# Gate blocks of a two-layer hybrid attention encoder: one run of blocks per attention job, or per pair of heads, in place of two

## The chip, the cores and the metric

One core of a Trainium2 chip runs the whole program. The metric is the device time of one execution in microseconds (us), given as the median of several runs. All times below are from the kernel before the change.

## The reference

Two layers (DEPTH = 2) over 640 tokens (512 of a prompt, 8 x 16 of samples with caches), D_MODEL = 1024. Cut to what matters here:

```python
h = rmsnorm(x, g_mix[l])
qa, ka, va, cq, ckv, kpe, ga, gb = jnp.split(h @ w_in[l], SPLIT_IDX, axis=-1)
oa = swa_sink_attention(...)          # branch A, window of 128, 8 heads
ob = mla_attention(...)               # branch B, latent attention, 8 heads
mixed = jax.nn.sigmoid(ga) * (oa @ w_oa[l]) + jax.nn.sigmoid(gb) * (ob @ w_ob[l])
x = x + mixed @ w_out[l]
x = x + (silu(h2 @ w_gate[l]) * (h2 @ w_up[l])) @ w_down[l]    # h2 = rmsnorm(x, g_ffn[l])
```

The columns `ga` and `gb` of the input projection, 2048 in all, are the gates. They depend on `h` alone, so their products can be computed at any time before the merge.

## The kernel before

Everything is float32. A large product is made of three fp32r products of a high and a low part (high x high, high x low, low x high). Tokens are the columns; 640 are taken as two halves of 320. A weight unit (128 output columns, 8 blocks of 128 rows) is loaded by SP into `w_raw`, rounded by ACT into `w_hi` (`high`, line 749), and the rest is left by POOL in `w_lo` (line 701); there are two slots of each. `high` of the next unit waits for `w_started`, which TensorE raises with the first matmul of the unit now in use (line 1347).

A gate group is one weight unit: 8 blocks (k = 0 to 7), each of 6 matmuls of 320 columns (lines 1336 to 1350), accumulated in `acc[:, 0]`. When all 8 blocks are done, `gate_full` lets DVE move the sum out (`gate_out`, line 1932), ACT takes the tanh (line 1009) and SP stores it. TensorE has 16 gate groups per layer. Most of them are cut up by hand and put between the steps of attention jobs, so that TensorE has work while the softmax of a job runs on DVE and ACT. `gate_part(j)` (line 119) says which blocks belong to job j:

- Window jobs (j = 0 to 15, branch A): 8 for the prompt with 4 blocks each, 8 for the samples with 2 blocks each.
- Head jobs (branch B on the prompt, 32 jobs, here numbered 0 to 31 from J_B = 16; job n is head n % 8 of the query tile t = n // 8, with (t + 1) x 128 keys): 2 blocks each in jobs 0 to 15, 1 block each in jobs 16 to 23, none in jobs 24 to 31. A gate group begins at jobs 0, 4, 8, 12 and 16 and ends at jobs 3, 7, 11, 15 and 23. Another whole group stands ahead of job 0.
- Sample jobs of branch B (8 jobs): 1 block each.

A job has four steps on TensorE: `score` (queries by keys, plain float32), `turn` (transposes the probabilities into the one buffer `psT`), the product with the values (`pv`, written in two halves of 64 output columns), and its gate blocks. Between them stand the other engines' steps:

- DVE: maximum of the scores (line 1913), then, when ACT has taken the exponential, the scaling of `probs` (line 1917). Its order is fixed: step n + 1's maximum with step n's scaling, and after the step of job n a `gate_out`, if a gate group ended in job n - 1.
- ACT, in this order for job n: exponential of job n + 1 (line 944), copy of `psT` to `pT` (line 954), copy of a finished output tile (line 959), tanh of an ended gate (line 1009), `high` of the next weight unit if a gate group begins in job n (line 758).

`turn` of job n waits for `probs` of job n and for the `pT` copy of job n - 1 (there is one `psT`). `pv` waits for the `pT` copy. The head jobs go in pairs: `pv_heads` does both jobs of a pair.

For window jobs, `jobs` (line 1352) puts half of a job's blocks ahead of its `pv` and half behind; where a gate group begins in the job, all stand behind `pv`. The sample jobs of branch B use the same function with 1 block: half rounded up is 1, so the block stands ahead of `pv`, or behind it in the first job. For head jobs, `head_jobs` (line 1376) runs, for the pair j and j + 1:

```python
score(j+4); gates(j); turn(j+1); score(j+5); gates(j+1); pv(j, j+1); turn(j+2)
```

Of the kernel before, what the change touches and what calls it, by code (L numbers as in the profile page):

```python
# [118 lines left out]
def gate_part(j):  # L119

    if j < J_SA:
        return 1 + j // 2, 4 * (j % 2), 4
    if j < J_B:
        return 1 + N_CHUNK // 2 + (j - J_SA) // 4, 2 * ((j - J_SA) % 4), 2
    if j < J_B + 2 * H_B:
        return GATE_B + 1 + (j - J_B) // 4, 2 * ((j - J_B) % 4), 2
    if j < J_B + 3 * H_B:
        return GATE_B + 5, j - J_B - 2 * H_B, 1
    if j >= J_SB:
        return GATES - 2, j - J_SB, 1  # L130
    return None
# [14 lines left out]
def gate_unit(g, block=0):  # L146


    if g < GATES_A:
        return N_IN + g  # L150
    return UNIT_GB + g - GATES_A + (g > GATE_SB or (g == GATE_SB and block >= KD // 2))


def gate_acc(g):

    return 1 if g in (GATES_A - 1, GATES - 1) else 0
# [117 lines left out]
def build(nc, io):  # L274
    with ExitStack() as ctx:
# [910 lines left out]
        def _(pe):  # L1186
            def unit_ready(n):
                pe.wait_ge(s_w_lo, n + 1)
# [76 lines left out]
            def score_b(l, j):  # L1265
                if j == J_B + 2:

                    pe.wait_ge(s_evac, l * TILES + (CREDIT + TILE_MERGE))
                if j - 4 >= (J_SB if j >= J_SB else J_B):

                    pe.wait_ge(s_exped, l * JOBS + (j - 3))
                if j < J_SB:
                    t, h = divmod(j - J_B, H_B)
                    last = pe.matmul(score_bank(j)[:, 0:(t + 1) * P], qB[0:QK_B, h, t * P:(t + 1) * P], kB[:, h, 0:(t + 1) * P],  # L1274
                                     start=True, stop=True, skip_group_check=True)
                else:
                    b = j - J_SB
                    cs = b % 4
                    pe.wait_ge(bcache_loaded[cs], l * (32 * DEC_BATCH // 4) + 32 * (b // 4 + 1))
                    pe.wait_ge(s_newcols, l * DEC_BATCH + (b + 1))  # L1280
                    out = score_bank(j)[:, 0:KEYS_B]
                    for a in range(KC):
                        pe.matmul(out, q_lat[:, a, b, :, :], cb_t[:, cs, a, :], start=a == 0, stop=False,
                                  skip_group_check=True)
                    last = pe.matmul(out, q_pe[:, b, :, :], cb_p[:, cs, :], start=False, stop=True, skip_group_check=True)
                last.then_inc(s_scored, 1)

            def turn_b(l, j):
                pe.wait_ge(s_probs, l * JOBS + (j + 1))
                if j >= 1:  # L1290
                    pe.wait_ge(s_pT, l * JOBS + j)
                s = j % 2
                n = (j - J_B) // H_B + 1 if j < J_SB else KC
                for i in range(n):
                    last = pe.transpose(psT[:, i * P:(i + 1) * P], probs[:, s, i * P:(i + 1) * P], ident[:, :])  # L1295
                if j >= J_SB:
                    last = pe.transpose(psT[0:DEC_SEQ, PAST:PAST + P], probs[:, s, PAST:KEYS_B], ident[:, :])
                last.then_inc(s_turned, 1)

            def pv_heads(l, j):  # L1300

                t, h = divmod(j - J_B, H_B)
                pe.wait_ge(s_pT, l * JOBS + (j + 2))
                if h == 0:
                    pe.wait_ge(s_o, l * O_GROUPS + (O_B + t))
                for i in range(t + 1):
                    for s in range(2):
                        r = slice(s * V_B, (s + 1) * V_B)
                        last = pe.matmul(psO[r, (h // 2) * P:(h // 2 + 1) * P], vB[:, i, (h + s) * V_B:(h + s + 1) * V_B],  # L1309
                                         pT[:, s, i * P:(i + 1) * P], start=i == 0, stop=i == t, skip_group_check=True)  # L1310
                        if i == t:
                            last.then_inc(s_pv, 1)
# [17 lines left out]
            def gate_blocks(l, g, blocks):  # L1330

                if blocks[0] == 0:

                    if g > 0:
                        pe.wait_ge(s_gate_evac, l * GATES + (g if gate_acc(g) == gate_acc(g - 1) else g - 1))
                for k in blocks:
                    slot = gate_unit(g, k) % 2
                    new = k == 0 or gate_unit(g, k) != gate_unit(g, k - 1)
                    if new:
                        unit_ready(l * UNITS + gate_unit(g, k))  # L1340
                    whi, wlo = w_hi[:, slot, k * P:(k + 1) * P], w_lo[:, slot, k * P:(k + 1) * P]
                    for w, x, s0, s1 in ((whi, h_hi, k == 0, False), (whi, h_lo, False, False), (wlo, h_hi, False, k == KD - 1)):
                        for half in range(2):
                            last = pe.matmul(acc[:, gate_acc(g), half, 0:HALF], w, x[:, k, half * HALF:(half + 1) * HALF],  # L1344
                                             start=s0, stop=s1)
                            if new:
                                last.then_inc(w_started, 1)
                                new = False
                if blocks[-1] == KD - 1:
                    last.then_inc(gate_full, 1)  # L1350

            def jobs(l, first, last, score, turn, pv, ahead, lead, blocks):
                for j in range(first, first + ahead):
                    score(l, j)

                gate_blocks(l, lead, blocks)
                if first == J_SB:
                    pe.wait_ge(s_sprep_c, l * 8 + 8)
                turn(l, first)
                for j in range(first, last):  # L1360
                    if j + ahead < last:
                        score(l, j + ahead)

                    g, k, n = gate_part(j) or (0, 0, 0)
                    before = (n + 1) // 2 if k else 0
                    if before:
                        gate_blocks(l, g, range(k, k + before))
                    pv(l, j)  # L1370
                    if n > before:
                        gate_blocks(l, g, range(k + before, k + n))
                    if j + 1 < last:
                        turn(l, j + 1)

            def head_jobs(l):

                for j in range(J_B, J_B + 4):
                    score_b(l, j)
                gate_blocks(l, GATE_B, range(KD))  # L1380
                turn_b(l, J_B)
                for j in range(J_B, J_SB, 2):
                    for e in (j, j + 1):
                        if j + 4 < J_SB:
                            score_b(l, e + 4)
                        g, k, n = gate_part(e) or (0, 0, 0)
                        if n:
                            gate_blocks(l, g, range(k, k + n))
                        if e == j:
                            turn_b(l, j + 1)  # L1390
                    pv_heads(l, j)
                    if j + 2 < J_SB:
                        turn_b(l, j + 2)
# [181 lines left out]
            for l in range(DEPTH):  # L1575
# [29 lines left out]
                pe.wait_ge(s_vprep_c, l * 4 + 4)  # L1605
                pe.wait_ge(acache_loaded, l * 32 + 32)
                jobs(l, J_A, J_B, score_a, turn_a, pv_a, 2, 0, range(3, KD))

                pe.wait_ge(s_cq, l * KQ + KQ)
# [47 lines left out]
                pe.wait_ge(s_spread, l * 16 + 16)  # L1657
                pe.wait_ge(s_kcopy, l * (H_B // 2) + H_B // 2)
                head_jobs(l)
                gate_blocks(l, GATE_SB, range(4))  # L1660

# [20 lines left out]

                pe.wait_ge(s_sprep_c, l * 8 + 6)
                jobs(l, J_SB, JOBS, score_b, turn_b, pv_b, 3, GATE_SB, range(6, KD))

                pe.wait_ge(uv_loaded, l * 16 + 16)
# [815 lines left out]
```

## Time and profile before

| | us |
|---|---|
| median of 3 runs | 1847.4 |
| runs | 1844.79 to 1848.89 |
| the profiled execution | 1847.09 |
| its span | 1845.3 |
| TensorE busy in the span | 1773.0 (96%) |
| window jobs with their gates, layer 0 | about 113.8 to 190 |
| head jobs with their gates, layer 0 | about 227 to 308 |
| head jobs, layer 1 | about 1131 to 1212 |

The span runs from the first to the last instruction of the profiled execution. The granted TensorE clock is full in the stretches looked at. Times in the rows are from the start of the span. "x2" after a matmul means two records; a plain float32 matmul leaves two, a transpose and an fp32r matmul one. The rows of 320-column matmuls come in twos, one row for the two halves; the start of a row minus the start of the row before is what the two took. A row's own length is longer than that, because matmuls overlap and their ends are modelled.

### The profile page before, as it was taken

The page shows a single profiled execution, that of the slowest core. Times are in us where ns is not written, and L with a number is a line of the kernel's source. Part 1 is how long each engine was busy: PE and PEld are TensorE (multiplying, and loading weights), DVE is VectorE, ACT ScalarE, POOL GpSimd, SP SyncE. Part 2 cuts the span into 40 slices and gives each one's busy share as a digit, 9 for nine tenths or more (in the row PEclk, how much of TensorE's full clock was granted, in tenths as well). Part 3 has the DMA queues.
Part 4 walks back from the last instruction along what each step waited for, and adds up shares of the span by engine and source line. Part 5 has one row for each costly group of instructions (what it writes and reads, how often), then busy time and mean ns, then how long its engine had stood idle before and what let it go on. Part 6 is the DMA issues. An engine that isn't in the chain of part 4 may idle for free.

```text
span 1845.3 us, 31477 instructions
## 1 busy us (share of the span) xinstructions
PE 1773.0 (96%) x12122; PEld 1695.9 (92%) x12122; DVE 1033.8 (56%) x1590; ACT 705.3 (38%) x1401; POOL 616.5 (33%) x345
## 2 busy tenths in 40 slices
PE   6899998999999999999999999999999999999998
PEld 6898886999989999999999888779999999999997
DVE  4464455475673746547537544545748545647464
ACT  4245345413442424334431643543134323334243
POOL 1322321133243443435233223112333443534432
PEclk9999999999999999999999999999999999999999
DMA  5222522342222121322222235134421231321212
GB/s 183 94 72 106 144 77 90 126 152 88 69 83 89 63 97 58 103 63 89 61 86 73 75 115 136 60 119 143 137 78 60 79 103 54 105 81 64 97 52 86
DMA packets 63786, 171.22 MB, mean 93 GB/s; under 512 B 8120, under 2 KB 13912, under 8 KB 63512
## 3 DMA queue, kind: packets, MB, share of 16 engines
q1 hardware_dynamic: 62808, 167.73, 27.9%
q10 hardware_dynamic: 864, 1.97, 0.3%
q8 instruction: 72, 1.18, 0.3%
q14 instruction: 42, 0.34, 0.1%
HBM read 151.03 MB, written 19.43 MB: 92 GB/s over the span
## 4 chain that ended last, share of the span: by engine, by line
PE 82%; DVE 7%; ACT 4%; issue 3%; POOL 2%; DMA 2%; SPq 1%; POOLq 0%; DVEq 0%; ACTq 0%
PE acc L1499 36%; PE acc L1344 12%; PE acc L1555 11%; PE psU L1555 9%; PE psS L1555 3%; PE psU L1295 1%; PE psU L1309 1%; POOL w_lo L706 1%; PE acc L1274 1%; PE psU L1324 1%; ACT w_hi L758 1%; ACT pT L954 1%; DVE s_lo L1952 1%; POOL w_lo L701 1%; PE acc L1652 1%
## 5 line engine op out<-in xcount | busy, mean ns | idle before, releaser
L701 POOL TENSOR_TENSOR w_lo<-w_raw,w_hi 128x1024 fp32r<-128x1024 f32 x102 | 249.2, 2443 | 696.6 <-ACT w_hi L758 696.6
L758 ACT ACTIVATE w_hi<-w_raw 128x1024 fp32r<-128x1024 f32 (+2 forms) x194 | 174.2, 898 | 449.6 <-PE acc L1499 414.5
L706 POOL TENSOR_TENSOR w_lo<-w_raw,w_hi 128x512 fp32r<-128x512 f32 (+2 forms) x92 | 143.9, 1564 | 340.4 <-ACT w_hi L758 340.4
L2288 DVE TENSOR_TENSOR xT<-acc,xT 128x640 f32<-128x640 f32 x88 | 72.6, 825 | 212.8 <-PE acc L1499 212.7
L1499 PE MATMUL acc<-act_hi,w_hi 128*128 128x320 f32 x694 | 159.4, 311 | 11.6 <-POOL w_lo L706 8.6
L1499 PE MATMUL acc<-act_hi,w_lo 128*128 128x320 f32 x694 | 158.2, 309 | 0.0
L1499 PE MATMUL acc<-act_lo,w_hi 128*128 128x320 f32 x694 | 158.1, 309 | 0.0
L725 POOL TENSOR_TENSOR s_raw<-w_raw 128x512 f32<-128x512 f32 x72 | 105.0, 1458 | 152.6 <-DVE s_lo L1952 110.0
L778 ACT ACTIVATE s_hi<-s_raw 128x512 fp32r<-128x512 f32 x144 | 90.3, 627 | 146.8 <-POOL s_raw L725 53.6
L1952 DVE TENSOR_TENSOR s_lo<-s_raw,s_hi 128x512 fp32r<-128x512 f32 x144 | 112.9, 799 | 48.1 <-ACT s_hi L778 47.7
L1344 PE MATMUL acc<-h_hi,w_hi 128*128 128x320 f32 x512 | 137.2, 349 | 1.2 <-DVE gate L1932 1.2
L1952 DVE TENSOR_TENSOR a_lo<-w_raw,a_hi 128x512 fp32r<-128x512 f32 x108 | 116.9, 1083 | 28.1 <-ACT a_hi L778 27.8
L1499 PE MATMUL acc<-h_hi,w_hi 128*128 128x320 f32 x512 | 120.0, 316 | 11.0 <-POOL w_lo L701 6.7
L1499 PEld LDWEIGHTS acc<-act_hi,w_hi 128*128 128x128 f32 x694 | 115.4, 188 | 14.6 <-POOL w_lo L706 10.7
L1499 PE MATMUL acc<-h_lo,w_hi 128*128 128x320 f32 x512 | 117.2, 310 | 0.0
L1499 PE MATMUL acc<-h_hi,w_lo 128*128 128x320 f32 x512 | 117.2, 310 | 0.0
L1344 PE MATMUL acc<-h_hi,w_lo 128*128 128x320 f32 x512 | 116.5, 309 | 0.0
L1344 PE MATMUL acc<-h_lo,w_hi 128*128 128x320 f32 x512 | 116.4, 308 | 0.0
L1499 PEld LDWEIGHTS acc<-act_hi,w_lo 128*128 128x128 f32 x694 | 115.9, 188 | 0.0
L1499 PEld LDWEIGHTS acc<-act_lo,w_hi 128*128 128x128 f32 x694 | 115.9, 188 | 0.0
L954 ACT ACTIVATE pT<-psU 128x256 f32<-128x256 f32 (+6 forms) x128 | 50.3, 406 | 147.2 <-PE psU L1295 84.8
L1344 PEld LDWEIGHTS acc<-h_hi,w_hi 128*128 128x128 f32 x512 | 84.6, 188 | 21.5 <-issue 10.7
(341 smaller groups left out, 4638.1 us busy)
## 6 DMA issues: line engine op xcount, KB each, us to landing
w_raw<-in_w SPq DMA_DIRECT2D x116, 512.0 KB, 3.5
w_raw<-in_w_pairs SPq DMA_DIRECT2D x72, 512.0 KB, 3.4
w_raw<-in_w SPq DMA_DIRECT2D x48, 256.0 KB, 2.7
gates<-gate SPq DMA_DIRECT2D x32, 320.0 KB, 2.2
tmp<-gates SPq DMA_DIRECT2D x32, 320.0 KB, 3.2
w_raw<-in_w SPq DMA_DIRECT2D x32, 320.0 KB, 2.8
cb_t<-in_cb_t SPq DMA_DIRECT2D x16, 256.0 KB, 3.0
cb_v<-in_cb_v SPq DMA_DIRECT2D x16, 256.0 KB, 2.8
```

Source lines behind the costliest of these rows:

```text
L701: pool.tensor_tensor(w_lo[:, s, :], w_raw[:, s, :], w_hi[:, s, :], ALU.subtract).then_inc(s_w_lo, 1)
L706: pool.tensor_tensor(w_lo[:, n % 2, 0:cols], w_raw[:, n % 2, 0:cols], w_hi[:, n % 2, 0:cols], ALU.subtract).then_inc(s_w_lo, 1)
L725: pool.tensor_tensor(part_raw[o][:, :], x, y, op).then_inc(s_sum, 1)
L758: act.activation(w_hi[:, slot, 0:cols], w_raw[:, slot, 0:cols], ACT.Copy).then_inc(s_w_hi, 1)
L778: act.activation(part_hi[o][:, :], part_source(i, o), ACT.Copy).then_inc(s_part_hi, 1)
L954: last = act.activation(pT[0:rows, j % 2, cols], psT[0:rows, cols], ACT.Copy)
L1274: last = pe.matmul(score_bank(j)[:, 0:(t + 1) * P], qB[0:QK_B, h, t * P:(t + 1) * P], kB[:, h, 0:(t + 1) * P], start=True, stop=True, skip ...
L1344: last = pe.matmul(acc[:, gate_acc(g), half, 0:HALF], w, x[:, k, half * HALF:(half + 1) * HALF], start=s0, stop=s1)
L1499: last = pe.matmul(acc[:, m % 2, half, 0:HALF], w, x[:, half * HALF:(half + 1) * HALF], start=s0, stop=s1)
L1555: last = pe.matmul(out, w, x[:, k, cols], start=fresh and s0, stop=s1, skip_group_check=True)
L1952: dve.tensor_tensor(part_lo[o][:, :], part_source(i, o), part_hi[o][:, :], ALU.subtract).then_inc(s_part_lo, 1)
L2288: then(evac, dve.tensor_tensor(two(xT[:, c, :]), acc2(m), two(xT[:, c, :]), ALU.add), alone=g is None and c == KD - 1)
```

## The change

In window jobs, all blocks of a job stand ahead of its `pv`, except in jobs where a gate group begins, where they stay behind it. In head jobs, both scores of the pair and the turn of the pair's second job come first, and the blocks of both jobs follow as one run ahead of `pv_heads`. The sample jobs of branch B keep their order: with one block, half rounded up is that block.

```diff
@@ jobs @@
                     g, k, n = gate_part(j) or (0, 0, 0)
-                    before = (n + 1) // 2 if k else 0
+                    before = n if k else 0
                     if before:
                         gate_blocks(l, g, range(k, k + before))
                     pv(l, j)
@@ head_jobs @@
                     for e in (j, j + 1):
                         if j + 4 < J_SB:
                             score_b(l, e + 4)
-                        g, k, n = gate_part(e) or (0, 0, 0)
-                        if n:
-                            gate_blocks(l, g, range(k, k + n))
-                        if e == j:
-                            turn_b(l, j + 1)
+                    turn_b(l, j + 1)
+                    parts = [gate_part(e) for e in (j, j + 1) if gate_part(e)]
+                    if parts:
+                        gate_blocks(l, parts[0][0], range(parts[0][1], parts[-1][1] + parts[-1][2]))
                     pv_heads(l, j)
                     if j + 2 < J_SB:
                         turn_b(l, j + 2)
```

A pair of head jobs is then: `score(j+4); score(j+5); turn(j+1); gates(j and j+1); pv(j, j+1); turn(j+2)`. Pairs 24 and 26 have no gates, but their second score now stands ahead of the second turn too.

## Rows read from the trace of the kernel before

**Rows 1.** The page's part 4: the chain that ended last, by engine.

```profile
PE 82%; DVE 7%; ACT 4%; issue 3%; POOL 2%; DMA 2%; SPq 1%; POOLq 0%; DVEq 0%; ACTq 0%
```

**Rows 2.** Timeline, head pair 14, layer 0: start, length, engine, line, operation, tiles.

```profile
267.59 0.45 PE L1344 MATMUL acc<-h_hi,w_lo 128*128 128x320 f32 x2
267.88 0.38 PE L1295 MATMUL psU<-ident,probs 128*128 128x128 f32 x2
268.10 0.81 PE L1274 MATMUL acc<-kB,qB 96*128 96x384 f32 x2
...
269.05 0.45 PE L1344 MATMUL acc<-h_lo,w_hi 128*128 128x320 f32 x2
...
270.21 0.46 PE L1344 MATMUL acc<-h_hi,w_lo 128*128 128x320 f32 x2
270.60 0.66 PE L1309 MATMUL psU<-pT,vB 128*64 128x128 f32 x8
271.19 0.55 PE L1295 MATMUL psU<-ident,probs 128*128 128x128 f32 x3
271.57 0.81 PE L1274 MATMUL psS<-kB,qB 96*128 96x384 f32 x2
```

**Rows 3.** Timeline, window job 1, layer 0: its pv between two runs of gates.

```profile
131.52 0.65 PE L1258 MATMUL psU<-pT,vwin 128*64 128x256 f32 x4
132.10 0.56 PE L1344 MATMUL acc<-h_hi,w_hi 128*128 128x320 f32 x2
132.49 0.45 PE L1344 MATMUL acc<-h_lo,w_hi 128*128 128x320 f32 x2
```

**Rows 4.** Timeline, head pair 0, layer 0, where a gate has just ended.

```profile
228.78 0.28 DVE L1917 TENSOR_SCALAR probs<-probs,rd 128x128 f32<-128x128 f32 x1
...
230.30 2.40 POOL L701 TENSOR_TENSOR w_lo<-w_raw,w_hi 128x1024 fp32r<-128x1024 f32 x1 [5.30 <-ACT w_hi L758]
...
230.72 2.06 DVE L1917 TENSOR_SCALAR probs<-probs,rd 128x128 f32<-128x128 f32 x1
...
232.84 0.33 PE L1295 MATMUL psU<-ident,probs 128*128 128x128 f32 x1
```

**Rows 5.** Timeline, window job 6, layer 0: a unit's first matmul and what follows it.

```profile
159.04 0.56 PE L1344 MATMUL acc<-h_hi,w_hi 128*128 128x320 f32 x2
...
159.55 1.06 ACT L758 ACTIVATE w_hi<-w_raw 128x1024 fp32r<-128x1024 f32 x1 [0.61 <-PE acc L1344]
...
160.69 2.41 POOL L701 TENSOR_TENSOR w_lo<-w_raw,w_hi 128x1024 fp32r<-128x1024 f32 x1 [8.87 <-ACT w_hi L758]
```

**Rows 6.** Timeline, head pairs 4 and 8, layer 0: second job's probs, next turn (its weight load, PEld, in pair 8).

```profile
238.53 0.28 DVE L1917 TENSOR_SCALAR probs<-probs,rd 128x128 f32<-128x128 f32 x1
...
242.79 0.33 PE L1295 MATMUL psU<-ident,probs 128*128 128x128 f32 x1
...
249.05 0.34 DVE L1917 TENSOR_SCALAR probs<-probs,rd 128x256 f32<-128x256 f32 x1
...
253.67 0.20 PEld L1295 LDWEIGHTS psU<-ident,probs 128*128 128x128 f32 x2 [0.35 <-DVE probs L1917]
```

**Rows 7.** Timeline, head pair 16, layer 0: weights, pv, next turn.

```profile
273.27 1.05 ACT L758 ACTIVATE w_hi<-w_raw 128x1024 fp32r<-128x1024 f32 x1
...
275.32 0.88 PE L1309 MATMUL psU<-pT,vB 128*64 128x128 f32 x12 [0.20 <-ACT pT L954]
...
277.19 0.55 PE L1295 MATMUL psU<-ident,probs 128*128 128x128 f32 x3 [1.00 <-DVE probs L1917]
```

**Rows 8.** Timeline, head pair 26, layer 0: no gates.

```profile
297.17 1.02 PE L1274 MATMUL acc<-kB,qB 96*128 96x512 f32 x2
297.37 0.60 ACT L954 ACTIVATE pT<-psU 128x512 f32<-128x512 f32 x1 [0.66 <-PE psU L1295]
...
298.12 0.63 PE L1295 MATMUL psU<-ident,probs 128*128 128x128 f32 x4
...
298.78 0.60 ACT L954 ACTIVATE pT<-psU 128x512 f32<-128x512 f32 x1
...
299.53 1.09 PE L1309 MATMUL psU<-pT,vB 128*64 128x128 f32 x16
```

## The prediction

> **What bounds the kernel now.** I read first the chain that ended last: TensorE holds 82% of it [rows 1], so a microsecond taken from or added to TensorE's own order counts nearly in full, and the other engines matter where TensorE waits for them. Then I read the timeline of the two stages that the change touches, for two questions: what does it cost TensorE to go from one kind of step to another, and what is ready when a step is brought forward?
>
> For the first question take pair 14 [rows 2]. Two matmuls of 320 columns take 0.29. The last two gate matmuls start at 267.59 and the turn at 267.88: leaving the gates for a turn costs nothing. The turn takes 0.22 (two transposes of 0.11). The score starts at 268.10, and the second row of gates at 269.05. Between them lie 0.95: the first two gate matmuls (0.29) and a score of 0.66. At one rate for four passes of 384 columns the score is about 0.64 (that makes 0.11 for 128 columns in a turn's two passes, as seen), so entering the gates from a score costs at most 0.02. Only pv costs: from the last gates (270.21) to pv is 0.39 where 0.29 would do, and from pv to the next turn 0.59 where the products themselves need 0.43. That turn then takes 0.38 to the next score, where three transposes need 0.32.
>
> In the window jobs pv stands between two runs of gates [rows 3]: pv takes 0.58, again 0.15 over its 0.43, and the first two gate matmuls behind it take 0.39, 0.10 too long.
>
> **Count.** A second run of gates disappears in 4 prompt and 6 sample window jobs and in 12 head pairs (0 to 22), 22 per layer, 44 in all. No matmul, transfer or copy is added or removed. SP's loads and stores keep their order and wait for the same signals, later by what is priced below; the next unit is needed about 10 us after its load, which hides that.
>
> **Window jobs: a small gain.** Their turns and scores keep their places; pv moves behind all gates of the job and is followed by a turn instead of gates. Removed: the 0.10 of entering the gates behind pv. Added: about 0.06 of a turn behind pv [rows 2]. The 0.15 behind pv itself stays. That is 0.04 a job; in 9 jobs per layer a turn follows (behind the last job comes another fp32r product, which pays the same entry), so 18 x 0.04 = 0.7 us gained. From below this could be 0; from above, if the whole 0.25 behind pv went, 4.5. I take 0.7, from the rows of the same steps. What covered the softmax is still there: from turn to turn a job has the same work as before, only in another order.
>
> The Trainium skill, page "TensorEngine Tiling (Array Packing)", section "Key Properties", says that a change of tiling mode drains TensorE. By that, pv with its 64-column halves has one change ahead of it and one behind in either order, so the window term would be 0 and the sum 4.6 in place of 3.9. The rows agree that the cost is at pv and not at gates, turns and full-width scores.
>
> **Head jobs: nothing gained, cover lost.** Here the removed boundary was gates to turn, score to gates: 0.02 at most by the rows. What changes is that turn(j+1) loses the 1.76 us (two blocks; 0.88 in jobs 16 to 23) that lay between it and turn(j). It must now wait for the pT copy of job j and for probs of job j+1, with only two scores as cover. Behind the waiting turn queue all gates of the pair and its pv; ACT's next w_hi waits for the first of those gates.
>
> In most pairs the scores suffice. A turn needs about 0.66 to reach the ACT copy at four transposes, the copy is 0.60, and the two scores of 512 columns that stand there take 1.71 [rows 8]; both sides shrink with t. In pair 2, with the shortest scores, up to 0.1 may show; it goes into the range.
>
> Where a gate has just ended, DVE does gate_out ahead of probs(j+1). Pairs 0, 4, 8, 12 and 16 are such.
>
> - Pair 0: probs(1) end at 229.06 [rows 4]. A waiting turn starts 0.06 behind probs (232.78 to 232.84 [rows 4]), so turn(1) starts at 229.12 and the gates at 229.23. Now a second chain: the first matmul of a unit lets ACT make the next w_hi 0.51 later and POOL finish w_lo 4.06 later (159.04 to 163.10 [rows 5]). The scaling of the job after next is held while POOL works: 2.06 instead of 0.28, ending 0.08 behind w_lo [rows 4]. So turn(j+2) comes no earlier than 4.06 + 0.08 + 0.06 = 4.20 behind the first gate: 233.43 instead of 232.84, **0.59** lost.
> - Pair 4: probs(5) end at 238.81 [rows 6], turn(5) 238.87, gates 238.98, turn(6) 243.18 instead of 242.79: **0.39**.
> - Pair 8: probs(9) end at 249.39, turn(9) 249.45, two transposes, gates 249.67. The POOL chain gives 253.87; TensorE's own way, four blocks (3.52), 0.10 to pv and 0.59, gives 253.88, instead of 253.67 [rows 6]: **0.21**. Less than the wait, because turn(10) was waiting 0.35 before.
> - Pair 12: the two scores are 1.28 instead of 0.85, 0.43 more, which covers a wait like pair 8's 0.4: **0**.
> - Pair 16: no wait at the turn: scores from 271.57 [rows 2] take 1.28, turn(17) is at 272.85, the gates begin at 273.18. But w_hi, at 273.27 before [rows 7], now waits until 273.18 + 0.51 = 273.69. Behind it on ACT stand the exponential of job 18 and the pT copy of job 17, so pv(16) and, through w_lo and probs, turn(18) come later by **0.42**. Both already waited [rows 7].
>
> Pair 26 has no gates. Its second score now stands ahead of turn(27): scores from 297.17, each 0.85, end at 298.87, where turn(27) began at 298.12. The copy follows 0.66 behind the turn and takes 0.60 [rows 8], so pT is ready at 300.13, pv starts at about 300.20 instead of 299.53: **0.67**. Jobs 28 to 31 have neither scores nor gates to make it up. In pair 24 ACT reaches the copy late anyway, behind a tanh: 0.
>
> Unknown is a score followed directly by a turn in the other pairs. Nearest is 297.17 to 298.12, 0.95 for 0.85 of work, so 0 to 0.10; but that turn also waited for the copy ending at 297.97. I take 0.
>
> **Sum.** Per layer 0.59 + 0.39 + 0.21 + 0.42 + 0.67 = 2.28, both layers 4.6, less 0.7: +3.9 us. Against the profiled execution's 1847.09 (span 1845.3) this is 1851.0. That execution lies 0.3 below the median of the runs shown, so I put the time at 1851.3. Bounds: the window term at 4.5 leaves +0.1; 0.10 in each of the nine other gated or unpriced pairs (2, 6, 10, 12, 14, 18, 20, 22, 24), both layers, adds 1.8: +5.7.
>
> **Rivals.**
> 1. The lost cover is largely taken up: the w_hi that begins a little later still finds POOL and DVE in time, and only pair 26 counts. 2 x 0.67 - 0.7 = +0.6, 1848.0. For it: turn(10) and turn(18) already waited for probs [rows 6, 7], so part of any delay ahead of them is free. Against: the delay goes into the very chain that they wait for.
> 2. Faster, through one mechanism: each second run of gates costs TensorE a restart like the one behind pv, 0.25, everywhere. 44 x 0.25 = 11.0, less 4.6: 1841.0. It wins from 4.6 / 44 = 0.10 per run. For it: rows 3. Against: in head pairs the rows show 0.02 at most, and 24 of the 44 are there.
> 3. More cover lost: a score directly ahead of a turn costs 0.10 in the nine pairs above: +5.7, 1853.1.
> That the change does nothing is no rival, except in the sample jobs of branch B, where no order changes.
>
> **How the numbers follow.** Forecast 0.62, rival 1 0.16, rival 2 0.08, rival 3 0.14. A measurement can tell about 0.2%, 3.7 us, from no change. The forecast of 3.9 lies on that bound: I count 0.36 of its 0.62 as slower and 0.26 as the same; with rival 3 slower is 0.50, with rival 1 the same is 0.42, faster 0.08. The range, 1846.0 to 1855.0, holds rivals 1 and 3 and the spread of the runs (4 us) at its ends, and leaves out rival 2.
>
> **What would show it.** Right: in pairs 0, 4 and 8 a turn(j+1) waiting 0.3 to 1.3 for probs; w_hi 0.51 behind the first gate in pairs 0 to 16; pv(26) about 0.7 later behind turn(26); window jobs 1, 3, 5 and 7 shorter by 0.04. Wrong: head pairs of equal length in both kernels, or window jobs shorter by 0.2 or more.

## The result and the profile after

| | us |
|---|---|
| before, median of 20 runs beside it | 1847.36 |
| after, median of 20 runs | 1849.87 |
| ratio after / before, 95% interval | 1.0015 (1.0008 to 1.0022) |
| after, profiled execution / its span | 1849.92 / 1848.1 |

The change costs 2.5 us by the medians; the interval reaches from 1.5 to 4.1. The forecast was +3.9. The page of the changed kernel has the same instructions and nearly the same chain as [rows 1]; one group stands out:

```profile
span 1848.1 us, 31477 instructions
PE 82%; DVE 7%; ACT 4%; issue 3%; POOL 2%; DMA 1%; SPq 1%; POOLq 0%; DVEq 0%; ACTq 0%
...
L1344 PE MATMUL acc<-h_hi,w_hi 128*128 128x320 f32 x512 | 125.7, 327 | 0.0
```

In the kernel before it was:

```profile
L1344 PE MATMUL acc<-h_hi,w_hi 128*128 128x320 f32 x512 | 137.2, 349 | 1.2 <-DVE gate L1932 1.2
```

The difference is the run that no longer restarts: 86 of these matmuls stand as the first of a run, 130 before, and the 44 between them are the count of the prediction. It is no gain of 11.5 us, because a row's length holds the overlap with what went before. So the page alone can't say where 2.5 us went; the timeline of the two stages can. I add up each stage from turn to turn, since a turn starts every pair:

| us per layer, after minus before | predicted | layer 0 | layer 1 |
|---|---|---|---|
| pair 0 | 0.59 | 0.69 (5.52 to 6.21) | 0.63 |
| pair 2 | 0 (up to 0.1 in the range) | 0.20 (4.70 to 4.90) | 0.18 |
| pair 4 | 0.39 | 0.33 (5.25 to 5.58) | 0.34 |
| pair 8 | 0.21 | 0.36 (5.75 to 6.11) | 0.35 |
| pair 16 | 0.42 | 0.33 (6.00 to 6.33) | 0.35 |
| pair 26 | 0.67 | 0.65 (3.88 to 4.53) | 0.64 |
| the other pairs | 0 | 0.00 each, within 0.01 | within 0.01 |
| head jobs, turn(0) to turn(30) | 2.28 | 2.57 | 2.49 |
| window jobs, turn(0) to turn(15) | -0.36 | -0.44 (65.65 to 65.21) | -0.66 (65.78 to 65.12) |

Both stages of both layers come to 2.57 + 2.49 - 0.44 - 0.66 = +3.96. The rest of the span, whose order no kernel here touches but for the blocks of window job 15 behind turn(15), was between 1555.5 and 1561.0 us in the eleven profiled executions of this study (span minus these stages).

One stretch of that rest does follow the order of the gates. From turn(15) of the window jobs to turn(0) of the head jobs it is 39.40 and 39.32 us (layers 0 and 1) in the kernel before, the same to 0.02 with the head part alone, and 39.20 to 39.23 in every kernel with the window part. Job 15's blocks end a gate group. Ahead of `pv` the group ends earlier, so the tanh, w_hi and w_lo behind it come earlier too, and TensorE no longer waits for w_lo in the product behind the window jobs. Layer 0, timeline, first the kernel before, then the changed one, where that wait is gone:

```profile
193.23 2.41 POOL L701 TENSOR_TENSOR w_lo<-w_raw,w_hi 128x1024 fp32r<-128x1024 f32 x1 [8.31 <-ACT w_hi L758]
...
195.69 0.30 PEld L1499 LDWEIGHTS acc<-cq_hi,w_hi 128*128 128x128 f32 x2 [0.26 <-POOL w_lo L701]
```

```profile
191.65 2.41 POOL L701 TENSOR_TENSOR w_lo<-w_raw,w_hi 128x1024 fp32r<-128x1024 f32 x1 [7.74 <-ACT w_hi L758]
```

With these 0.20 and 0.11 the change comes to +3.65 us. The stages are the finer measure, and the ratios agree with them within their intervals; most ratios lie below the stages' sums, by up to 1.7 us, and what makes up the difference is not shown.

Pair 0 of the changed kernel, timeline, to be read against [rows 4]:

```profile
226.17 0.82 DVE L1931 TENSOR_TENSOR gate<-acc,rstd 128x640 f32<-128x640 f32 x1 [6.25 <-PE acc L1344]
...
227.43 0.28 DVE L1916 TENSOR_SCALAR probs<-probs,rd 128x128 f32<-128x128 f32 x1
...
227.77 0.33 PE L1295 MATMUL psU<-ident,probs 128*128 128x128 f32 x1 [1.07 <-DVE probs L1916]
...
227.87 0.53 PE L1344 MATMUL acc<-h_hi,w_hi 128*128 128x320 f32 x2
...
228.34 1.06 ACT L758 ACTIVATE w_hi<-w_raw 128x1024 fp32r<-128x1024 f32 x1 [0.58 <-PE acc L1344]
...
229.64 2.40 POOL L701 TENSOR_TENSOR w_lo<-w_raw,w_hi 128x1024 fp32r<-128x1024 f32 x1 [5.98 <-ACT w_hi L758]
...
230.05 2.07 DVE L1916 TENSOR_SCALAR probs<-probs,rd 128x128 f32<-128x128 f32 x1
...
232.18 0.33 PE L1295 MATMUL psU<-ident,probs 128*128 128x128 f32 x1 [0.19 <-DVE probs L1916]
```

Read it from the top: DVE moves the ended gate out, then scales probs(1); turn(1) waits 1.07 for it; the gates begin 0.10 behind that turn; w_hi follows 0.47 behind the first gate; POOL works from 229.64 to 232.04; the scaling of job 2 is held meanwhile (2.07) and ends 0.08 behind POOL; turn(2) starts 0.06 later. Each link is one that the prediction named.

Pair 16, timeline, against [rows 7]:

```profile
273.36 0.54 PE L1344 MATMUL acc<-h_hi,w_hi 128*128 128x320 f32 x2
273.85 1.06 ACT L758 ACTIVATE w_hi<-w_raw 128x1024 fp32r<-128x1024 f32 x1 [0.23 <-PE acc L1344]
...
275.14 2.34 POOL L701 TENSOR_TENSOR w_lo<-w_raw,w_hi 128x1024 fp32r<-128x1024 f32 x1 [9.94 <-ACT w_hi L758]
...
275.90 0.88 PE L1309 MATMUL psU<-pT,vB 128*64 128x128 f32 x12 [0.53 <-ACT pT L954]
276.03 1.67 DVE L1916 TENSOR_SCALAR probs<-probs,rd 128x384 f32<-128x384 f32 x1
...
277.76 0.55 PE L1295 MATMUL psU<-ident,probs 128*128 128x128 f32 x3 [0.98 <-DVE probs L1916]
```

w_hi waits for the first gate (0.23), pv waits for the copy behind w_hi on ACT (0.53, 0.20 before), turn(18) waits for the held probs (0.98, 1.00 before): the delay at the head of the chain passes through to its end.

Pair 26, timeline, against [rows 8]:

```profile
297.74 1.88 PE L1274 MATMUL acc<-kB,qB 96*128 96x512 f32 x4
...
299.46 0.60 PE L1295 MATMUL psU<-ident,probs 128*128 128x128 f32 x4
...
300.10 0.60 ACT L954 ACTIVATE pT<-psU 128x512 f32<-128x512 f32 x1 [0.89 <-PE psU L1295]
...
300.75 1.09 PE L1309 MATMUL psU<-pT,vB 128*64 128x128 f32 x16 [0.69 <-ACT pT L954]
```

Both scores stand ahead of turn(27), and pv waits 0.69 for the copy that follows the turn. In the old order the second score lay between them.

A sample job of the window stage, job 10, first in the kernel before, then in the changed one:

```profile
175.61 0.34 PE L1261 MATMUL psU<-pT,va_c 80*64 80x64 f32 x4
175.88 0.56 PE L1344 MATMUL acc<-h_hi,w_hi 128*128 128x320 f32 x2
176.27 0.46 PE L1344 MATMUL acc<-h_lo,w_hi 128*128 128x320 f32 x2
...
176.86 0.27 PE L1246 MATMUL psU<-ident,probs 128*80 128x128 f32 x1
177.06 0.34 PE L1229 MATMUL psS<-ka_c,qA 64*64 64x64 f32 x4
```

```profile
175.64 0.34 PE L1261 MATMUL psU<-pT,va_c 80*64 80x64 f32 x4
175.91 0.31 PE L1246 MATMUL psU<-ident,probs 128*80 128x128 f32 x1
176.14 0.34 PE L1229 MATMUL psS<-ka_c,qA 64*64 64x64 f32 x4
```

pv takes 0.27 to the next step in both. Before, the first two gates behind it take 0.39 where 0.29 is the rate, and the turn behind the gates 0.20; after, the turn behind pv takes 0.23. So 0.10 less 0.03: 0.07 a job. That is the term of the prediction, somewhat larger in this sample job than the 0.04 priced from a prompt job.

### The profile page after: what moved, and what is told of

It is laid out like the page before. It is cut to its first block, busy times and chain, and to the rows that moved or that the text cites. A ratio compares the mean times of both kernels' runs of the same rounds, so it can differ in the third digit from the quotient of the medians.

```text
span 1848.1 us, 31477 instructions
## 1 busy us (share of the span) xinstructions
PE 1771.8 (96%) x12122; PEld 1695.2 (92%) x12122; DVE 1031.5 (56%) x1590; ACT 706.2 (38%) x1401; POOL 617.3 (33%) x345
## 4 chain that ended last, share of the span: by engine, by line
PE 82%; DVE 7%; ACT 4%; issue 3%; POOL 2%; DMA 1%; SPq 1%; POOLq 0%; DVEq 0%; ACTq 0%
PE acc L1498 36%; PE acc L1344 11%; PE acc L1554 11%; PE psU L1554 9%; PE psS L1554 3%; PE psU L1295 1%; PE psU L1309 1%; PE acc L1274 1%; POOL w_lo L706 1%; PE psU L1324 1%; ACT w_hi L758 1%; ACT pT L954 1%; DVE s_lo L1951 1%; POOL w_lo L701 1%; PE acc L1651 1%
## 5 line engine op out<-in xcount | busy, mean ns | idle before, releaser
L1498 PE MATMUL acc<-h_hi,w_hi 128*128 128x320 f32 x512 | 119.7, 315 | 9.0 <-POOL w_lo L701 6.6
L1344 PE MATMUL acc<-h_hi,w_hi 128*128 128x320 f32 x512 | 125.7, 327 | 0.0
```

Source lines behind the costliest of these rows:

```text
L1498: last = pe.matmul(acc[:, m % 2, half, 0:HALF], w, x[:, half * HALF:(half + 1) * HALF], start=s0, stop=s1)
```

## The experiments

"Stages" is the sum over the window and head jobs of both layers against the kernel before, from the traces; it is the sum that the table above gives as +3.96, without the stretch behind the window jobs (0.3 us less in every kernel with the window part).

| kernel | stages, us | ratio to before (95%) | median, us |
|---|---|---|---|
| the change | +3.96 | 1.0015 (1.0008 to 1.0022) | 1849.87 |
| window part alone | -1.07 | 0.9991 (0.9982 to 1.0000) | 1845.82 |
| head part alone | +5.09 | 1.0027 (1.0016 to 1.0037) | 1850.98 |
| change, ungated pairs as before | +2.64 | 1.0009 (1.0000 to 1.0018) | 1848.02 |
| change, weights one job later | +1.08 | 1.0002 (0.9993 to 1.0011) | 1848.36 |
| change, gate moved out one step later | +1.16 | 1.0000 (0.9991 to 1.0009) | 1848.09 |
| change, weights two jobs later | +0.34 | 1.0000 (0.9991 to 1.0009) | 1848.05 |
| window part, old heads, weights two later | -3.62 | 0.9978 (0.9969 to 0.9988) | 1843.84 |
| one run where a group begins, both late | -4.78 | 0.9975 (0.9965 to 0.9985) | 1840.66 |
| the same, tanh one job later | -5.90 | 0.9959 (0.9945 to 0.9972) | 1837.55 |

The kernel before had a median of 1847.36 beside the change, 1847.55 beside the next four kernels, 1847.53 beside the three after them and 1845.38 beside the last two, so the ratio is what compares them. In each row the ratio's interval holds the stages' sum.

**Window part alone.**

```diff
-                    before = (n + 1) // 2 if k else 0
+                    before = n if k else 0
```

> Only the window jobs' part of the change; head jobs as in the kernel before. My theory: a job without its second run of gates saves the entry into the gates behind pv (0.10 us) and pays 0.06 for a turn behind pv, so the window jobs shorten by 0.4 to 0.8 us per layer, 0.8 to 1.6 in all: ratio to the kernel before about 0.9993, 1846 us; head pair 0 takes 5.52 and pair 26 takes 3.88, as before. Rival (every run of gates costs a restart of 0.25 us): 18 merged jobs save 4.5 us, 1843, ratio 0.9976, each odd window job and each sample job shorter by 0.25.

Measured: 65.20 and 65.12 us in the two layers, as in the changed kernel to 0.01, and head pairs as before to 0.02; 0.9991. The rival of 0.25 for every run falls: the sample stage, turn(8) to turn(15), shortens by 0.24 and 0.46 with five jobs merged in it (the sixth, job 15, lies behind it), where the rival asks for 1.25.

**Head part alone.** The head hunk of the change, with the window line as it was.

```diff
-                    before = n if k else 0
+                    before = (n + 1) // 2 if k else 0
```

> Only the head jobs' part of the change; window jobs as in the kernel before. My theory: the whole loss is here, 2.3 to 2.6 us per layer: +4.6 to +5.1, 1852.2 us, ratio about 1.0026; turn to turn 6.2 in pair 0, 5.6 in pair 4, 6.1 in pair 8, 6.3 in pair 16, 4.5 in pair 26, and the pairs 6, 10, 14 and 18 to 22 as before. Rival (the changed kernel's later stages account for the difference, the heads' loss being given back behind them, where the sample jobs wait for their own inputs): head pairs longer as named, but the time within 0.1% of before.

Measured: 6.20, 4.90, 5.59, 6.10, 6.33 and 4.53 us in pairs 0, 2, 4, 8, 16 and 26, nothing else moved; 1.0027. The whole loss is in the head jobs, and it is not given back behind them.

**Ungated pairs as before.** Where a pair has no gates, the second score goes behind the second turn again.

```diff
+                    if gate_part(j):
...
+                    else:
+                        for e in (j, j + 1):
+                            if j + 4 < J_SB:
+                                score_b(l, e + 4)
...
+                            if e == j:
+                                turn_b(l, j + 1)
```

> The changed kernel, but the pairs 24, 26, 28 and 30, which have no gates, keep the old order (the second score behind the second turn). My theory: pair 26 goes from 4.53 back to 3.88 us, since turn(27) and with it the pT copy are 0.85 earlier, and nothing else changes: 0.65 per layer, 1.3 less than the changed kernel, 1848.6 us. Rival (pv of pair 26 is held by something else, the exponential or the copies of ACT): pair 26 stays at 4.5 us and the time at 1849.9.

Measured: pair 26 takes 3.88 in both layers, nothing else changes. The timeline shows the turn early and pv nearly without a wait:

```profile
298.88 0.63 PE L1295 MATMUL psU<-ident,probs 128*128 128x128 f32 x4
299.35 1.02 PE L1274 MATMUL acc<-kB,qB 96*128 96x512 f32 x2
299.55 0.60 ACT L954 ACTIVATE pT<-psU 128x512 f32<-128x512 f32 x1
...
300.30 1.09 PE L1309 MATMUL psU<-pT,vB 128*64 128x128 f32 x16
```

**Weights one job later.** The order of the change; only ACT's rounding of the next unit moves.

```diff
-                    if gate_started(j) is not None:
-                        high(l, gate_unit(gate_started(j)) + 1)
+                    begun = j - 1 if lead == GATE_B else j
+                    if begun >= first and gate_started(begun) is not None:
+                        high(l, gate_unit(gate_started(begun)) + 1)
```

> The changed kernel, but in the head jobs ACT rounds the next gate unit (w_hi) one job later than the one in which the group begins, behind the pT copy of that second job; POOL's w_lo follows. My theory (the chain first gate, w_hi, w_lo, held probs sets turn(j+2) in pairs 0, 4, 8 and 16): probs(j+2) are done before POOL begins and no longer take 2.1 but about 0.3 us; pair 16 goes from 6.33 to 5.0 us or less, since pv no longer waits behind w_hi (0.53) nor turn(18) for probs (0.98), pair 0 from 6.2 to about 5.9, pair 4 from 5.6 to 5.4, pair 8 from 6.1 to 5.9: 1.5 to 2.2 per layer, 3 to 4.4 less than the changed kernel, about 1846. Rival 1 (the probs that follow, of job j+3, are held in their place and stop turn(j+3)): pairs 0, 4, 8 and 16 shorter but the pairs 2, 6, 10 and 18 longer by as much, time 1849.9. Rival 2 (turn(j+2) waits for what the second job's turn and probs left late, not for POOL): pairs 0, 4 and 8 within 0.1 of the changed kernel, only pair 16 shorter.

Measured, layer 0: pair 0 from 6.21 to 5.94, pair 4 from 5.58 to 5.48, pair 8 from 6.11 to 6.00, pair 16 from 6.33 to 4.67; but pair 18 from 4.67 to 5.31. Pair 16's turns, timeline:

```profile
275.32 1.08 ACT L758 ACTIVATE w_hi<-w_raw 128x1024 fp32r<-128x1024 f32 x1
275.64 0.41 DVE L1917 TENSOR_SCALAR probs<-probs,rd 128x384 f32<-128x384 f32 x1
...
276.63 2.35 POOL L701 TENSOR_TENSOR w_lo<-w_raw,w_hi 128x1024 fp32r<-128x1024 f32 x1 [10.48 <-ACT w_hi L758]
...
276.99 0.55 PE L1296 MATMUL psU<-ident,probs 128*128 128x128 f32 x3
...
277.52 1.67 DVE L1917 TENSOR_SCALAR probs<-probs,rd 128x384 f32<-128x384 f32 x1
...
279.25 0.55 PE L1296 MATMUL psU<-ident,probs 128*128 128x128 f32 x3 [0.42 <-DVE probs L1917]
```

The probs of job 18 are now scaled in 0.41, ahead of POOL's work; turn(18) starts without a wait. The probs of job 19 are the held ones instead (1.67), and turn(19) waits 0.42. So the chain from gate to w_hi to w_lo to probs is shown, and rival 1 is right for pair 18 alone: 1.66 gained, 0.64 given back. In pairs 0, 4 and 8 the hold was 0.27, 0.10 and 0.11 of the loss, so for pairs 4 and 8 rival 2 was nearly right; the rest is something else. In all, the stages are 2.9 below the changed kernel, where I had expected 3 to 4.4.

**Gate moved out one step later.**

```diff
-                    if j == first:
+                    late = 1 if lead == GATE_B else 0
+                    if j - late == first:
                         gate_out(l, lead)
-                    elif gate_ended(j - 1) is not None:
-                        gate_out(l, gate_ended(j - 1))
+                    elif j - late > first and gate_ended(j - late - 1) is not None:
+                        gate_out(l, gate_ended(j - late - 1))
```

> The changed kernel, but in the head jobs DVE moves an ended gate out one step later, so the scaling of job j+1 (probs) no longer stands behind it where a group begins. The longest single wait that the changed order shows, turn(1) for probs 1.07 us, should vanish, and so the waits of turn(5) and turn(9). My theory (those waits cost little by themselves: the next group's gates need the moved-out sum and the w_hi, w_lo, probs chain runs on from them): in pair 0 the gates now wait for the move instead, beginning at most 0.1 earlier, the tanh and w_hi follow it, and turn(2) stays where it is: pair 0 6.1 to 6.4, pair 4 5.5 to 5.9, pair 8 6.0 to 6.3, time 1849.9 or up to 1 more. Rival (the wait for probs is the loss itself): pair 0 shorter by 0.7 to 1.0 and pairs 4 and 8 by 0.2 to 0.3, 2.5 to 3 in all, 1847.2.

Here my theory fell and the rival was right: pair 0 takes 5.52, pair 4 5.23, pair 8 5.75, which is what they took before the change (in all 2.8 less than the changed kernel). The timeline of pair 0:

```profile
225.92 0.27 PE L1295 MATMUL psU<-ident,probs 128*128 128x128 f32 x1
...
226.12 0.82 DVE L1931 TENSOR_TENSOR gate<-acc,rstd 128x640 f32<-128x640 f32 x1 [5.38 <-PE acc L1344]
...
226.65 0.30 PE L1295 MATMUL psU<-ident,probs 128*128 128x128 f32 x1
...
227.00 0.30 PEld L1344 LDWEIGHTS acc<-h_hi,w_hi 128*128 128x128 f32 x2 [0.24 <-DVE gate L1931]
...
227.63 1.04 ACT L758 ACTIVATE w_hi<-w_raw 128x1024 fp32r<-128x1024 f32 x1
```

I had taken it that the move, now behind probs(1), would start later. It does not: DVE stands idle before it, 5.38 us here and 6.25 in the changed kernel, waiting for the lead group to end. The inputs of probs(1) were there, so the scaling and the maximum ahead of it (6.25 - 5.38 = 0.87) go into the idle stretch, and the move starts as early as before (0.20 behind turn(0) in both). The gates begin 1.08 behind turn(0) instead of 1.90, and w_hi, w_lo and turn(2) follow.

**Weights two jobs later.**

```diff
-                    if gate_started(j) is not None:
-                        high(l, gate_unit(gate_started(j)) + 1)
+                    begun = j - 2 if lead == GATE_B else j
+                    if begun >= first and gate_started(begun) is not None:
+                        high(l, gate_unit(gate_started(begun)) + 1)
```

> The changed kernel, but in the head jobs ACT rounds the next gate unit two jobs later than the one in which the group begins (one later gave 2.4 to 2.9 us and cost 0.6 of it again in pair 18). My theory: POOL's w_lo now falls where probs have two steps in hand, so the held probs stop no turn: pair 16 at 4.67 us and pair 18 at 4.67 too, pairs 0, 4 and 8 as with one job later (5.94, 5.48, 6.00): 1.2 less than that kernel, 1847.1 us or ratio 0.9996. Rival (the hold only moves on by a job: turn(j+3) or turn(j+4) waits for it): pair 18 at 5.2 or more, or pairs 2, 6 and 10 longer than 4.90, 5.13 and 5.56, time 1848.4 or above.

Measured: pair 16 at 4.67, pair 18 at 4.91 (layer 1: 4.84), pairs 0, 4 and 8 as with one job later. Half right: the hold falls on probs of job 20, and turn(20) still waits a little:

```profile
279.56 2.39 POOL L701 TENSOR_TENSOR w_lo<-w_raw,w_hi 128x1024 fp32r<-128x1024 f32 x1 [8.62 <-ACT w_hi L758]
...
280.46 1.71 DVE L1917 TENSOR_SCALAR probs<-probs,rd 128x384 f32<-128x384 f32 x1
...
282.22 0.55 PE L1296 MATMUL psU<-ident,probs 128*128 128x128 f32 x3 [0.18 <-DVE probs L1917]
```

The stages give 0.74 less than with one job later, where I had expected 1.2.

**Window part, old heads, weights two jobs later.** Head jobs in the order of the kernel before.

```diff
-                    before = (n + 1) // 2 if k else 0
+                    before = n if k else 0
...
-                    if gate_started(j) is not None:
-                        high(l, gate_unit(gate_started(j)) + 1)
+                    begun = j - 2 if lead == GATE_B else j
+                    if begun >= first and gate_started(begun) is not None:
+                        high(l, gate_unit(gate_started(begun)) + 1)
```

> The window jobs' part of the change alone (head jobs in the order of the kernel before), with w_hi of the next gate unit two jobs later in the head jobs. If the order of before is the better one and POOL's hold is a cost of its own that both orders pay: pair 16 from 6.00 to 4.7 us (its pv no longer behind w_hi, turn(18) no longer behind w_lo), pair 8 from 5.75 to 5.4 (the 0.35 that turn(10) waited), pairs 0 and 4 0 to 0.1 shorter: 1.7 per layer, 3.4 in all, with the window jobs' 1.2: 4.6 below the kernel before, 1842.9 us, ratio 0.9975. Rival (the old order's second score and gates already hid the hold, apart from what turn(10) and turn(18) show at the end, and another wait follows): pair 16 stays above 5.5 and the ratio is that of the window part alone, 0.999.

Measured: pair 16 at 4.67, pair 8 at 5.57, pair 18 at 4.90 (0.24 longer: the hold falls there), the rest as before: 3.6 less than the kernel before, where I had expected 4.6, and 0.9978. The hold was a cost in the old order too, nearly all of it in pair 16. Pair 0 stays at 5.50: its limit there is not POOL but the first gate, which waits 0.58 for the sum to be moved out of `acc`, with one score as its only cover:

```profile
227.39 0.27 PE L1296 MATMUL psU<-ident,probs 128*128 128x128 f32 x1
...
228.47 0.56 PE L1345 MATMUL acc<-h_hi,w_hi 128*128 128x320 f32 x2 [0.58 <-DVE gate L1933]
```

The first gate stands 1.08 behind turn(0), as with the late move above; but the second score and a turn still follow behind it.

**One run where a group begins.** The change's order in pairs 0, 4, 8, 12 and 16, the old order in the others, the gate moved out one step later, the weights two jobs later and in the group of pair 16 three. The cut is against the changed kernel; the hunk that moves the gate out is the one shown above.

```diff
+                    if gate_started(j) is not None:
...
+                        turn_b(l, j + 1)
+                        parts = [gate_part(e) for e in (j, j + 1) if gate_part(e)]
...
+                    else:
+                        for e in (j, j + 1):
...
+                            if e == j:
+                                turn_b(l, j + 1)
...
-                    if gate_started(j) is not None:
-                        high(l, gate_unit(gate_started(j)) + 1)
+                    begun = j if lead != GATE_B else j - (3 if j >= J_B + 2 * H_B else 2)
+                    if begun >= first and gate_started(begun) is not None:
+                        high(l, gate_unit(gate_started(begun)) + 1)
```

> The window part; in the head jobs the one run of gates of the change only in the pairs where a group begins (0, 4, 8, 12, 16), the order of before in the others; the moved-out gate one step later on DVE; w_hi of the next unit two jobs later, three in the group of pair 16. Theory (with both late steps out of its way, the new order is worth its cover where DVE has to move a gate out first, and costs a copy wait elsewhere): pair 0 at 5.2 us (gates 1.08 behind turn(0), 3.72 to pv, 0.37 to turn(2)) against 5.50 in the old order, pair 2 at 4.70, pair 4 at 5.15, pair 8 at 5.56, pair 16 and 18 at 4.67, pair 26 at 3.88: about 0.6 per layer less than the old order with late weights, 1842.6, ratio 0.9971. Rival (the new order costs as such, whatever the other engines do): pairs 0 and 4 not below 5.50 and 5.24, time 1843.8 or more, ratio 0.9978 or above.

Measured: pair 0 5.16, pair 2 4.72, pair 4 5.13, pair 8 5.56, pairs 16 and 18 4.67 and 4.66, pair 26 3.88; stages 1.16 less than with the old heads. So the changed order is no loss as such. Where a group begins it puts two scores and a turn between the lead group's end and the next group's first gate, so that of the 0.58 that this gate waits for the move in the old order 0.24 is left, as with the late move above; in pair 0 that gives 0.34 against 5.50. It loses where its turn stands in front of the cover. The two ratios, 0.9975 and 0.9978, can't be told apart; the stages can.

**The tanh one job later too.** The cut is against the kernel just shown.

```diff
-                    if j == first:
+                    late = 1 if lead == GATE_B else 0
+                    if j > first:
+                        out(l, j - 1)
+                    if j - late == first:
                         sigmoid(l, lead)
-                    else:
-                        out(l, j - 1)
-                        if gate_ended(j - 1) is not None:
-                            sigmoid(l, gate_ended(j - 1))
+                    elif j - late > first and gate_ended(j - late - 1) is not None:
+                        sigmoid(l, gate_ended(j - late - 1))
```

> The kernel with one run of gates where a group begins, and besides ACT's tanh of an ended gate one job later in the head jobs, behind the pT copy of the second job. Theory (pv of pair 24 waits 0.8 us for a pT copy that stands behind the tanh of 0.74): pair 24 from 4.64 to 3.9 to 4.0 us and nothing else longer: 1.2 to 1.4 less, 1841.3, ratio 0.9964. Rival (the tanh then delays the exponentials of jobs 27 and 28, and the wait moves to pair 26): pair 24 shorter, pairs 26 and 28 longer by as much, same time.

Measured: pair 24 from 4.63 to 4.02 in layer 0 (4.63 to 4.01 in layer 1), pair 26 from 3.88 to 3.92. It has the lowest ratio of all, 0.9959; its interval overlaps that of the kernel just shown, and the stages, 1.12 less, tell the two apart. ACT in pair 24, first with the tanh in its place, then one job later:

```profile
290.25 0.74 ACT L1009 ACTIVATE gate<-gate 128x640 f32<-128x640 f32 x1
...
291.54 0.60 ACT L954 ACTIVATE pT<-psU 128x512 f32<-128x512 f32 x1
```

```profile
291.30 0.61 ACT L954 ACTIVATE pT<-psU 128x512 f32<-128x512 f32 x1
...
291.78 0.76 ACT L1009 ACTIVATE gate<-gate 128x640 f32<-128x640 f32 x1
```

Counted from the copy ahead of it (289.28 and 289.67), the pT copy of job 25 comes 0.63 earlier.

## Why the prediction was right

**Sign and size.** +3.9 was forecast, +3.96 is what the stages show, +3.65 with the stretch behind the window jobs, and +2.5 (1.5 to 4.1) what the runs show. That the sums agree to 0.3 is partly luck: in layer 0 pairs 0, 2 and 8 cost 0.45 more than priced, pairs 4, 16 and 26 0.17 less, and the window part gained twice its price.

**Count and place.** TensorE's own order is what counts: it holds the same 82% of the chain as in [rows 1], and each loss in the table stands at a wait of TensorE.

**Window jobs.** Right in sign and kind, half the size: 0.04 a job was priced, 0.36 per layer; 0.44 and 0.66 came in the stage, and 0.20 and 0.11 behind it. In jobs 1, 3 and 5 the price holds: turn to turn they are 0.10 shorter and the jobs behind them 0.07 longer, since a turn's own cost falls into the job that it starts. The sample jobs 10, 11, 13 and 14 are 0.06 to 0.11 shorter; their pv and turn are smaller shapes than the prompt rows that I priced from [rows 2, 3]. In layer 1 another 0.16 stands in job 12, which is not merged: in the kernel before its pv takes 0.46 to the next step there, 0.27 in layer 0, and no run shows why. Behind job 15 I had seen that the next product pays the same entry (its first two matmuls take 0.41), but not that the group, and with it the next w_lo, would be done earlier. The Trainium skill, page "TensorEngine Tiling (Array Packing)", section "Key Properties", has TensorE drained at a change of tiling mode, which by itself made this term 0: the trace shows a gain instead, and the measurement decides. What the order of steps changes is the cost of entering fp32r gates, 0.10, against that of entering a turn, 0.03 to 0.06.

**Pairs 0, 4 and 8.** The chain was right, and two runs each took one link out. Its length I took as 4.06 + 0.08 + 0.06 = 4.20 from [rows 4, 5], for all three pairs; from the first gate to turn(j+2) it is 4.31 in pair 0, 4.15 in pair 4 and 4.39 in pair 8. Two links differ. POOL starts 0.24, 0.07 and 0.23 behind the end of w_hi in these pairs, 0.08 in [rows 5]. And the scaling, which ends 0.08 behind POOL for the 128 columns of pairs 0 and 4, ends 0.15 behind it for the 256 columns of pair 8. That is 0.69 for 0.59, 0.33 for 0.39 and 0.36 for 0.21. Pair 4 of the changed kernel, to be read against the same two rows of pair 0 above:

```profile
238.99 1.06 ACT L758 ACTIVATE w_hi<-w_raw 128x1024 fp32r<-128x1024 f32 x1 [0.58 <-PE acc L1344]
...
240.12 2.40 POOL L701 TENSOR_TENSOR w_lo<-w_raw,w_hi 128x1024 fp32r<-128x1024 f32 x1 [8.09 <-ACT w_hi L758]
```

What I had not seen is how the two causes stand together: I named the chain as what sets turn(j+2), and it does, but it starts from a wait that was avoidable, DVE's move of the ended gate in front of probs. The late weights alone return 0.27 of pair 0's 0.69, the late move alone all of it.

**Pair 2.** Priced at 0 with 0.1 in the range; 0.20 and 0.18 came. By the trace turn(3) waits for the single `psT`, with two scores of 128 keys as cover: the copy of job 2 ends at 232.82 and turn(3) starts at 232.96, 0.14 later. With the late move turn(1) of pair 0 also starts 0.14 behind the copy of its first job. I underestimated a step that I had named. The kernels with the old order there take 4.72; the copy itself was not changed in a run.

**Pair 12, and the scores ahead of a turn.** 0 in both cases, as taken: pairs 6, 10, 14 and 18 to 24 are equal to 0.01.

**Pair 16.** Right in mechanism, 0.33 for 0.42. Moving the weights showed how much more was there: 1.66 in the changed order, 1.33 in the old one. [rows 7] showed both of these waits, 0.20 and 1.00, in the kernel before.

**Pair 26.** 0.65 for 0.67, and undone where the pair keeps the old order.

**Rivals.** Rival 1 (delay absorbed) falls, since pairs 0, 4, 8 and 16 are longer. Rival 2 (0.25 a run) falls with the window part alone and with the head pairs that stay equal. Rival 3 falls with the pairs 6, 10, 14 and 18 to 24.

**POOL and DVE.** The 2.07 of a scaling that takes 0.28 alone, ending 0.08 behind POOL, agrees with a lock and not with shared bandwidth. The Trainium skill says so: "SBUF — State Buffer", section "SBUF: two separate sides", calls the pair of ports of these two engines an exclusive lock held for a whole instruction. The run with the weights one job later agrees: 0.41 where POOL was idle, 1.67 for the next scaling, under POOL's 2.35. The held scalings of all widths agree too: they end 0.08, 0.15 and 0.22 behind POOL for 128, 256 and 384 columns (pairs 0, 8 and 16), and alone they take 0.28, 0.34 and 0.41. Each further 128 columns cost 0.07 behind POOL, as much as alone, which fits columns that are moved only once POOL is done.

## What to carry to other kernels

A block of cover work belongs between an operation and the step that waits for its result; merging two blocks into one moves one of those steps out from behind its cover, so price every step that is moved forward by what must be ready for it, on every engine and not on TensorE alone. Where an in-order queue stands idle for a signal, look at what is queued behind the waiting instruction: here one gate moved out, one rounding and one tanh, each one to three jobs later, with the merged order kept only where a group begins, took the stages from +3.96 to -5.90. And when the stage that an edit touches repeats to 0.03 us from run to run while the rest of the program varies by several, compare stages, and look at the stretch right behind them too.

## What was not expected of the hardware

The late move of the gate was the one miss of kind: a wait of 1.07 us that I held to be covered by a chain behind it was itself the start of that chain. Entering fp32r matmuls costs 0.10 us behind a pv, yet at most 0.02 behind a full-width score by the sum of [rows 2]; no run here tells which property of the step before decides it. Behind a sample job's score, which uses 64 rows and columns, the first two take 0.40 from start to start (174.54 to 174.94 in the kernel before), but that count can't be set against the 0.02: behind the full-width score of [rows 2] it is larger still, because the first of them starts while the score runs.

And POOL's start behind the end of w_hi alternates from unit to unit, in window and head jobs of every kernel here alike: 0.23 to 0.24 in one and 0.07 to 0.08 in the next in layer 0, 0.16 and 0.08 in layer 1. The loop in which POOL makes w_lo (lines 697 to 701) takes two units a pass. In the trace the slow units have four instructions of POOL's sequencer between the end of w_hi and the start of w_lo in layer 0 and two in layer 1, the fast units one. [rows 5] showed a fast unit; pairs 0, 8 and 16 have slow ones. No run changed that loop.
